# Attention: the pieces of the row maximum as pairs of 64 array rows each, one fold fewer on GpSimd, and the first copy of the row sums on ScalarE

## The reference

```python
def blocked_attention(q, k, v):          # 8 query heads, 2 key heads, head size 64
    qb = ... q in blocks of 128 rows ... * (Dh ** -0.5)
    def one_block(qi):
        s = jnp.einsum('bqhgd,bkhd->bhgqk', qi, k)     # latent: 2048 own keys + 256 cached
        p = jax.nn.softmax(s, axis=-1)
        return jnp.einsum('bhgqk,bkhd->bqhgd', p, v)
```

## Time and profile before

| | before |
|---|---|
| median of 3 runs | 3383.89 us (3378.5 to 3384.28) |
| the profiled execution | 3377.92 us, its span 3376.2 us |
| granted TensorE clock, mean | 0.971 |
| TensorE busy in the span | 3177.5 us (94%) |
| VectorE | 2378.0 us (70%) |
| ScalarE | 1713.6 us (51%) |
| GpSimd | 1710.5 us (51%) |

### The profile page before, as it was taken

How to read it: one execution, slowest core, us unless ns; L and a number is a source line. 1 busy time by engine, 2 the same in 40 slices (tenths; PEclk the granted TensorE clock), 3 DMA queues, 4 the chain that set the end, 5 groups by cost and what they waited for, 6 DMA issues and landing times. The chain is left out here.

```text
span 3376.2 us, 48426 instructions
## 1 busy us (share of the span) xinstructions
PE 3177.5 (94%) x18066; PEld 2778.3 (82%) x18066; DVE 2378.0 (70%) x3262; ACT 1713.6 (51%) x2475; POOL 1710.5 (51%) x910
## 2 busy tenths in 40 slices
PE   6988999999998799998899699999999999899998
PEld 5975777777776797887688699999999999688886
DVE  4877999999996575339633588988888987222367
ACT  5865888888887685221244433344444333211122
POOL 2655999999997011111023377756766774000001
PEclk8998999999998899999999899999999999899999
DMA  6432011111100444338575567757785775555466
GB/s 217 156 121 76 28 49 45 51 44 47 49 21 24 141 154 144 109 97 260 174 226 183 184 202 229 238 163 245 230 246 156 225 221 158 191 200 183 175 254 224
DMA packets 431529, 518.42 MB, mean 154 GB/s; under 512 B 40112, under 2 KB 322048, under 8 KB 431296
## 3 DMA queue, kind: packets, MB, share of 16 engines
q1 hardware_dynamic: 384224, 412.21, 38.4%
q10 hardware_dynamic: 43968, 91.86, 7.9%
q0 software_dynamic: 3104, 11.27, 0.8%
HBM read 341.62 MB, written 173.64 MB: 153 GB/s over the span
## 5 line engine op out<-in xcount | busy, mean ns | idle before, releaser
L781 POOL TENSOR_TENSOR att_tlo<-att_prob,att_thi 128x1024 fp32r<-128x1024 f32 x292 | 694.0, 2405 | 62.7 <-ACT att_thi L950 62.7
L166 PE MATMUL fu_p<-fu_hhi,fu_whi 128*128 128x384 f32 x1848 | 619.5, 335 | 28.5 <-PEq L111 18.5
L168 PE MATMUL fu_p<-fu_hhi,fu_wlo 128*128 128x384 f32 x1848 | 618.6, 335 | 0.0
L167 PE MATMUL fu_p<-fu_hlo,fu_whi 128*128 128x384 f32 x1848 | 618.5, 335 | 0.0
L945 ACT ACTIVATE att_prob<-att_p_s 128x512 f32<-128x512 f32 x584 | 341.4, 592 | 86.7 <-PE att_p_s L841 80.8
L166 PEld LDWEIGHTS fu_p<-fu_hhi,fu_whi 128*128 128x128 f32 x1848 | 348.0, 188 | 31.5 <-issue 18.8
L993 DVE TENSOR_REDUCE att_mx<-att_p_r 128x1 f32<-128x512 f32 x512 | 341.4, 683 | 44.4 <-PE att_p_r L805 43.3
L167 PEld LDWEIGHTS fu_p<-fu_hlo,fu_whi 128*128 128x128 f32 x1848 | 347.9, 188 | 0.0
L168 PEld LDWEIGHTS fu_p<-fu_hhi,fu_wlo 128*128 128x128 f32 x1848 | 347.8, 188 | 0.0
L950 ACT ACTIVATE att_thi<-att_prob 128x1024 fp32r<-128x1024 f32 x292 | 309.8, 1061 | 9.3
L1807 POOL TENSOR_TENSOR fu_wsum<-fu_ws 128x1024 f32<-128x1024 f32 x66 | 178.7, 2708 | 233.9 <-DMA fu_ws<-in_w_ffn_dram 124.1
(11 more groups left out here) (361 smaller groups left out, 8045.0 us busy)
## 6 DMA issues: line engine op xcount, KB each, us to landing
fu_ws<-in_w_ffn_dram SPq DMA_DIRECT2D x132, 512.0 KB, 8.3
gated_d<-fu_out SPq DMA_DIRECT2D x99, 448.0 KB, 5.8
fd_src<-gated_d SPq DMA_DIRECT2D x63, 704.0 KB, 4.2
second_d<-fu_hs ACTq DMA_DIRECT2D x77, 512.0 KB, 3.3
fu_hs<-in_w_ffn_dram ACTq DMA_DIRECT2D x121, 256.0 KB, 4.2
fd_second<-second_d SPq DMA_DIRECT2D x40, 512.0 KB, 5.9
fd_w<-second_d SPq DMA_DIRECT2D x37, 512.0 KB, 5.3
ga_h<-hT_d SPq DMA_DIRECT2D x36, 512.0 KB, 4.2
```

Source lines behind the costliest of these rows:

```text
L166: pe.matmul(out, ah, bh, start=first, stop=False)
L167: pe.matmul(out, ah, bl, start=False, stop=False)
L168: return pe.matmul(out, al, bh, start=False, stop=last)
L781: pool.tensor_tensor(tlo[:, sl, :], prob[:, sl, :], thi[:, sl, :].bitcast(F32), ALU.subtract).then_inc(s.lo, 1)
```

## The change

Three things. First, a third copy of queries: `qc` holds the queries' high part in rows 64 to 127 (a third load in each unit), and a piece is now a product over 64 rows, high part of the queries with high part of the keys: even pieces in rows 0 to 63 (`qa`), odd pieces in rows 64 to 127 (`qc`). The low part of the queries is no longer in the maximum; the softmax divides by a sum made with the same maximum, so its result doesn't depend on it. `PLAN` has even numbers, and the pieces of a step come in pairs directly behind one another, after values(0). Second, `FOLDED` loses step 6: GpSimd folds once in a unit, and VectorE adds both halves of step 6. Third, the first copy of the sums goes from VectorE to ScalarE, where it stands in step 1 ahead of the exponentials; VectorE then only has the second half of step 0 to add.

```diff
-    PLAN = [3, 2, 1, 2, 2, 3, 3, 0, 0]
+    PLAN = [2, 2, 2, 2, 2, 4, 2, 0, 0]
-    FOLDED = (2, 6)
+    FOLDED = (2,)
...
+        qc = ph.sb("qc", [P, Q_SLOTS, ROW], F32R)
...
                     sp.dma_start(qb[0:HD, v.q, :].bitcast(F32), src[0:HD, :]).then_inc(s.q[v.q], 16)
+                    sp.dma_start(qc[HD:P, v.q, :].bitcast(F32), src[0:HD, :]).then_inc(s.q[v.q], 16)
...
                     if before:
                         pe.wait_ge(*before)
+                    rows = slice(i % 2 * HD, (i % 2 + 1) * HD)
+                    queries = (qa, qc)[i % 2]
                     if v.nds > 1 and i < G4 * FULL:
                         h, c = i // FULL, i % FULL
-                        pe.matmul(bank[:, :], qa[:, v.q, h * P:(h + 1) * P], g.keysT[:, v.kv, 0, c * ROW:(c + 1) * ROW],
+                        pe.matmul(bank[:, :], queries[rows, v.q, h * P:(h + 1) * P], g.keysT[rows, v.kv, 0, c * ROW:(c + 1) * ROW],
                                   start=True, stop=True).then_inc(s.piece, 1)
...
                     if S.val:
                         values(0)
-                    if pieces:
-                        piece(*pieces.pop(0))
+                    for p in pieces[0:2]:
+                        piece(*p)
+                    pieces = pieces[2:]
                     if S.now:
                         scores(1)
-                    if len(pieces) > 1:
-                        piece(*pieces.pop(0))
                     if S.val:
                         values(1)
                     for p in pieces:
                         piece(*p)
...
+                    if S.sum and S.sum[1] == 0:
+                        b, j = S.sum
+                        act.wait_ge(s.ex, b.g0 * 2 + 1)
+                        wait(act, s.sums_out, b.n)
+                        act.activation(p_sum[:, :], prob[:, b.step_no[0] % SLOTS_P, 0:ROW], ACT.Copy).then_inc(s.sum, 1)
...
-                    if i == 0 and j == 0:
-                        wait(dve, s.sums_out, b.n)
-                        dve.tensor_copy(p_sum[:, :], half).then_inc(s.sum, 1)
-                    else:
-                        dve.wait_ge(s.sum, done)
-                        dve.tensor_tensor(p_sum[:, :], p_sum[:, :], half, ALU.add).then_inc(s.sum, 1)
+                    dve.wait_ge(s.sum, done)
+                    dve.tensor_tensor(p_sum[:, :], p_sum[:, :], half, ALU.add).then_inc(s.sum, 1)
...
                         for i in range(1 if b.nds > 1 and j in FOLDED else 2):
-                            add(b, j, i)
+                            if i or j:
+                                add(b, j, i)
```

More of the change, by code:

```diff
@@ L573, in attention @@
     N_PIECES = G4 * FULL + G4 // 2
-    PLAN = [3, 2, 1, 2, 2, 3, 3, 0, 0]
-    PLAN_FIRST = [3, 2, 1, 2, 2, 3, 3, 2, 0]
+    PLAN = [2, 2, 2, 2, 2, 4, 2, 0, 0]
+    PLAN_FIRST = [2, 2, 2, 2, 2, 4, 2, 2, 0]
     AHEAD = 2
-    FOLDED = (2, 6)
+    FOLDED = (2,)
     BANKS = 3
@@ L799, in piece @@
                     if i == 0:
-                        pe.wait_ge(s.q[v.q], v.q_round * 32 + 32)
+                        pe.wait_ge(s.q[v.q], v.q_round * 48 + 48)
                     if before:
                         pe.wait_ge(*before)
+                    rows = slice(i % 2 * HD, (i % 2 + 1) * HD)
+                    queries = (qa, qc)[i % 2]
                     if v.nds > 1 and i < G4 * FULL:
                         h, c = i // FULL, i % FULL
-                        pe.matmul(bank[:, :], qa[:, v.q, h * P:(h + 1) * P], g.keysT[:, v.kv, 0, c * ROW:(c + 1) * ROW],
+                        pe.matmul(bank[:, :], queries[rows, v.q, h * P:(h + 1) * P], g.keysT[rows, v.kv, 0, c * ROW:(c + 1) * ROW],
                                   start=True, stop=True).then_inc(s.piece, 1)
@@ L810, in piece @@
                         for n in range(2):
-                            last = pe.matmul(bank[:, n * 2 * P:(n + 1) * 2 * P], qa[:, v.q, (h0 + n) * P:(h0 + n + 1) * P],
-                                             g.keysT[:, v.kv, 0, k0:k0 + 2 * P], start=True, stop=True)
+                            last = pe.matmul(bank[:, n * 2 * P:(n + 1) * 2 * P], queries[rows, v.q, (h0 + n) * P:(h0 + n + 1) * P],
+                                             g.keysT[rows, v.kv, 0, k0:k0 + 2 * P], start=True, stop=True)
                         last.then_inc(s.piece, 1)
@@ L835, in scores @@
                             pe.wait_ge(s.aux, e.n + 1)
-                            pe.wait_ge(s.q[e.q], e.q_round * 32 + 32)
+                            pe.wait_ge(s.q[e.q], e.q_round * 48 + 48)
                         wait(pe, s.ex, half - (BANKS - 1))
```

## The result

| | before | after |
|---|---|---|
| median of 3 runs | 3383.89 us | 3541.59 us (3529.78 to 3548.09) |
| ratio after / before | | 1.0469, 95% interval 1.045 to 1.0487 |
| profiled execution (span) | 3377.92 (3376.2) us | 3529.78 (3528.0) us |
| unit of attention, mean of 28 | 24.38 us | 29.46 us |

The change makes the kernel 4.7% slower, 158 us. The direction was forecast (0.84), the size was not: 101 us were forecast, and 3541.59 lies above the range (3395 to 3520). The unit is read from the starts of the adaLN products, as in the earlier trace rows, here over 14 distances of two units each.

The account below looks back on a forecast made before the run. The prediction took four nearly full engines and the order of waits within a unit as the bound. Pairs and three waits added 3.4 us a unit, 109 us over 32 units; it said 3485 us, range 3395 to 3520.

Parts of the forecast that it names:

- The cost of a pair: TensorE in attention: 0.63 us a pair against 0.47 for two full pieces; nine pairs add 1.4 us a unit.
- rows 9: Trace of linear attention's 64-row products: halves start together, and going in and out of 64 rows costs 0.40 us.
- R3: Rival: no cost of going over in attention, but the waits; 3387 us, no change; chance 0.06.
- R4: Rival: pairs cost 0.23 us, waits are absorbed and GpSimd bounds the unit; faster, 3346 us; chance 0.10.
- R2: Rival: halves do not overlap at 512 columns, a pair costs 0.87 us; 3553 us; chance 0.08.
- The three waits: Second halves wait for the reciprocal (step 3, +0.85 us), qb (step 8, +0.9), VectorE's reduction (step 5, +0.45) per unit.
- R1: Rival: the going over is paid, the waits are not; unit 25.8 us, 3429 us; chance 0.16.
- I count it at nothing: ScalarE's added copy in step 1, 0.6 us a unit, is covered by its wait for scores; otherwise 19 us.
- The clock: Attention: all engines read at the full granted clock, 2.4 GHz; no term for a fall.
- The sum: Per unit 1.4 + 0.85 + 0.9 + 0.45 = 3.6 us, taken as 3.4; times 32 units, 109 us.
- The range: Whole kernel: 3395 to 3520 us, leaving out the faster case, the no-change case and the end of the no-overlap case.

Follow-up runs that it names:

- run 14: Changed kernel, with five extra, overwritten products over 128 rows ahead of the step 3 pair to fill TensorE's idling: 3506.96 us, ratio 1.0377.
- run 13: Changed kernel with pairs over the full 128 rows and extra full-height products filling TensorE's idling in step 3: 3474.89 us, ratio 1.0292.
- run 2: Kernel before, with its pieces made 64-row products (third load of queries) standing singly in their old places: 3558.13 us, ratio 1.0512.
- run 5: Changed kernel with pairs only: GpSimd's second fold and VectorE's first copy of the sums restored: 3515.66 us, ratio 1.0392.
- run 10: Changed kernel with only the pair of step 8 moved behind values(1): 3526.58 us, ratio 1.0425.
- run 1: Changed kernel with its pairs over the full 128 rows instead of 64, same order and places: 3498.06 us, ratio 1.0336.
- run 8: Changed kernel with only the pair of step 3 moved behind values(1): 3487.93 us, ratio 1.0315.
- run 9: Changed kernel with the first 64-row half of step 3's pair computed six times to fill TensorE's idling: 3522.82 us, ratio 1.0418.

## Why the prediction was wrong

- *The cost of a pair* (0.63 us; rows 9 carried over to another stage): right as read, 0.63. Its effect on the unit was 1.0 us (run 14 less run 13), not 1.4. From the last values product ahead of a pair to the second product of scores behind it, five of the nine pairs take 0.16 us more in run 14 than in run 13, just as forecast, and two take 0.2 more. But the one of step 3 takes 0.12 less, and the last one of step 5 takes the same or 0.2 less: there the chain of the wait sets the end, and the going over takes place inside the wait. R3 and R4 fall with the 0.63. R2 falls because a pair costs no more than a lone half (0.62, run 2).
- *The three waits*: all at the places named, each for the reader named. The halves start 1.63 us apart in step 3 where 1.06 was forecast, 1.30 in step 8 for about 1.0, and 0.83 in step 5, as forecast. In step 3 the excess is the copy's: without it they start 1.04 apart (run 5). In step 8 it is not, since run 5 has 1.3 there too. Order and copy together cost 27.46 - 24.38 = 3.1 us a unit (run 13). The copy cost 0.54 by itself and 0.3 beside the pairs, so 2.5 to 2.8 are left for the order, against the 2.2 of the forecast. R1 (waits absorbed) falls.
- *"I count it at nothing" for ScalarE's copy*: wrong, and it was wrong in the case that the prediction priced itself at 0.6 us a unit. Measured 0.54 alone. "ScalarE has time in hand by the wait for scores" was true of the unit (73.7 us of such waits in 310 to 1040 us, 2.5 a unit), but not of steps 1 and 2, where that wait is 0.16 us, and these carry the chain to the reciprocal.
- *The clock*: this is the step that failed, a term left out. The prediction read 1.00 in the stage of before, kept that for the changed kernel, and let TensorE idle a microsecond more in step 3 without asking what that does to the clock. The runs show 1.03 us a unit, 33 us. With the clock held up and all else kept (run 14) the kernel takes 3507 us, inside the range.
- *The sum*: 3.4 us a unit forecast. Measured: 2.5 order, 0.5 copy, 1.0 going over, 1.0 clock, 5.1 in all with rounding. Without clock and copy it would have been 3.5. That this is so near 3.4 is in part luck: the order was sized 0.3 too low and the going over 0.4 too high. The clock and the copy (33 and some 16 us) made most of the miss of 57 us. The other 8 us are a slip of the forecast: its own 109 us on top of the median of 3383.89 give 3493, not 3485.
- *The range* left the clock and the copy out, though the copy's 19 us stood in the text.

## What to carry to other kernels

A shared pair of banks is a queue: before two users are put side by side, look whose reader each of them waits for and what that reader's chain is. Slack of an engine must be read in the steps on the chain, not over the loop; and a new wait on TensorE, of half a microsecond or more, has to be priced with the clock that may fall behind it. Two 64-row products side by side pay only if several pairs share one going over: one pair costs 0.63 us against 0.47 for two full products. By the same figures two pairs behind one another would take 0.87 against 0.93; this is an estimate that no run here tests.

## What the runs showed of the hardware that was not expected

The granted clock fell to half, mostly for 3.4 us at a time, in an otherwise dense stage: behind idle gaps of only 1.1 us (changed kernel, run 10), 1.65 us (run 1) and even 0.55 us (run 5) in step 3, and not behind gaps of 0.8 and 1.0 us in step 8 (runs 8, 1 and 13). So the gap's length alone does not tell. Filling the gap with products over 128 rows removed all of these stretches (runs 13 and 14), filling it with products over 64 rows removed 7 of 15 (run 9). A weight load is not hidden across a change of height: the first product behind a change reads 0.50 us instead of 0.40, and each change costs about 0.1 us more, since that product also starts 0.33 instead of 0.23 us behind the one before. It is so in attention (606.06 to 607.16) just as in linear attention.
